# Router logits with the weights stationary on two halves of TensorE's columns, in a hybrid decoder layer

## The reference, cut to what matters

```python
x = x + h                                    # h: the mixer's output, @ w_out
xn = rms_norm(x, norm_ffn)
p_group = softmax(x32 @ w_router_group + b_router_group)     # 4 groups
fine = x32 @ w_router_expert + b_router_expert               # 32 experts
...                                          # best group, best two experts of it, their gates
```

## Time and profile before

| what | value |
|---|---|
| median of 3 runs | 1838.29 us (1837.46 to 1838.7) |
| the profiled execution | 1837.38 us, its span 1835.7 us |
| PE busy | 1771.8 us, 97% of the span |
| DVE busy | 1151.4 us, 63% |
| ACT busy | 863.1 us, 47% |
| chain that ended last, PE's share of the span | 36%, of it L2379 1% |

### The profile page before, as it was taken

How to read it: one execution, slowest core, us unless ns; L and a number is a source line. 1 busy time by engine, 2 the same in 40 slices (tenths; PEclk the granted TensorE clock), 3 DMA queues, 4 the chain that set the end, 5 groups by cost and what they waited for, 6 DMA issues and landing times. The chain is left out here.

```text
span 1835.7 us, 28478 instructions
## 1 busy us (share of the span) xinstructions
PE 1771.8 (97%) x9926; PEld 1529.7 (83%) x9926; DVE 1151.4 (63%) x1954; ACT 863.1 (47%) x1554; POOL 485.7 (26%) x495
## 2 busy tenths in 40 slices
PE   7989999999999999999999999979999999999997
PEld 6878888999999888888878978758888888888883
DVE  5267665311111354545456556689999999999985
ACT  5255555311111223332223223358787778778873
POOL 3022332000000232323231112223965333333320
PEclk9989999999999999999999999979999999999998
DMA  7121211332213203030204643279999999999987
GB/s 225 54 50 43 56 47 47 94 93 65 76 52 95 69 27 92 23 94 23 95 1 132 192 142 124 91 286 381 396 385 384 392 387 385 383 383 387 384 338 292
DMA packets 149531, 333.30 MB, mean 182 GB/s; under 512 B 33712, under 2 KB 103008, under 8 KB 123792
## 3 DMA queue, kind: packets, MB, share of 16 engines
q1 hardware_dynamic: 127408, 278.19, 41.7%
q0 software_dynamic: 21376, 53.27, 8.4%
q10 hardware_dynamic: 672, 0.85, 0.3%
HBM read 304.24 MB, written 46.35 MB: 191 GB/s over the span
## 5 line engine op out<-in xcount | busy, mean ns | idle before, releaser
L2832 POOL DMA_INDIRECT y_d<-e_y,e_idxs x32 | 138.4, 4325 | 201.4 <-DVE e_y L2938 179.8
L2909 DVE TENSOR_TENSOR e_Lg<-e_rawg,e_Hg 128x1024 fp32r<-128x1024 f32 x128 | 148.3, 1219 | 8.3 <-ACT e_Hg L2858 8.3
L2909 DVE TENSOR_TENSOR e_Lu<-e_rawu,e_Hu 128x1024 fp32r<-128x1024 f32 x128 | 147.8, 1213 | 0.0
L2909 DVE TENSOR_TENSOR e_Ld<-e_rawd,e_Hd 128x1024 fp32r<-128x1024 f32 x124 | 143.1, 1213 | 0.0
L2858 ACT ACTIVATE e_Hg<-e_rawg 128x1024 fp32r<-128x1024 f32 x128 | 124.7, 1051 | 9.2 <-DMA e_rawg<-in_w_gate 9.2
L2858 ACT ACTIVATE e_Hu<-e_rawu 128x1024 fp32r<-128x1024 f32 x124 | 121.0, 1059 | 0.0
L2858 ACT ACTIVATE e_Hd<-e_rawd 128x1024 fp32r<-128x1024 f32 x124 | 120.7, 1051 | 0.0
L164 PE MATMUL bank<-r_wH,xH 128*128 128x512 f32 x256 | 105.9, 414 | 2.4 <-DVE r_gs L1512 2.4
L164 PE MATMUL bank<-e_Hg,e_xH 128*128 128x512 f32 x256 | 100.8, 394 | 3.5 <-DVE e_xL L2915 3.5
L164 PE MATMUL bank<-e_Hu,e_xH 128*128 128x512 f32 x256 | 102.8, 402 | 0.0
L166 PE MATMUL bank<-r_wH,xL 128*128 128x512 f32 x256 | 101.5, 397 | 0.0
(11 more groups left out here) (464 smaller groups left out, 4774.6 us busy)
## 6 DMA issues: line engine op xcount, KB each, us to landing
e_rawg<-in_w_gate SPq DMA_DIRECT2D x64, 1024.0 KB, 8.6
e_rawu<-in_w_up SPq DMA_DIRECT2D x64, 1024.0 KB, 7.5
e_rawd<-in_w_down SPq DMA_DIRECT2D x62, 1024.0 KB, 8.1
raw<-in_w_in SPq DMA_DIRECT2D x51, 512.0 KB, 4.0
c_Y<-y_d SPq DMA_DIRECT2D x8, 1024.0 KB, 12.2
m_t<-b_m_s POOLq DMA_DIRECT2D x8, 528.0 KB, 3.4
m_gate<-gate_t POOLq DMA_DIRECT2D x8, 528.0 KB, 4.0
m_m<-m_t POOLq DMA_DIRECT2D x8, 528.0 KB, 3.9
```

What stands on the lines that cost most here:

```text
L2832: pool.indirect_dma_start(out=ch.y_d, out_offset=bass.IndirectOffsetOnAxis(ap=idx[:, e % IDX, 1:2], axis=0), in_=y[:], in_offset=None, bou ...
L2909: dve.tensor_tensor(L[kind][:, q], raw[kind][:, q], H[kind][:, q].bitcast(F32), ALU.subtract).then_inc(w_lo[kind], 1)
```

## The change

The roles in the router product are swapped. The weights `wr`, padded from 40 to 64 columns, are stationary, and the turned tokens move (128 columns). The eight slices of the contraction go in turn to the lower and the upper half of the columns (`PART`), so bank 6 holds two partial sums of the transposed logits, of the even slices in partitions 0 to 63 and of the odd ones in 64 to 127. ScalarE copies them to SBUF (`parts_out`). A new step `join` on PE multiplies them by `halves`, two identities of 40 columns one above the other (rows 0 to 39 and 64 to 103), which adds the halves and turns the logits back to one row a token. DVE reads them from another place of bank 6. In the loop the join stands behind two more slices of the projection, and two slices follow it. The waits for `r_mm` that guarded the turned rows are for `part_mm` now.

```diff
-        wr, rb = sb("o_wr", [P, KT, NL]), sb("o_rb", [P, NL])
+        wr, rb = sb("o_wr", [P, KT, P // 2]), sb("o_rb", [P, NL])
...
+        parts, halves = aside("o_parts", [P, P]), aside("o_halves", [P, NL])
+        PART = [slice(r * P // 2, (r + 1) * P // 2) for r in range(2)]
...
+            def parts_out(t):
+                m = rows_of(t)
+                act.wait_ge(part_mm, t + 1)
+                act.activation(parts[:, 0:m], banks[6][:, 0:m], ACT.Copy).then_inc(part_out, 1)
...
             for t in range(1, NT):
                 back(t - 1)
+                parts_out(t - 1)
                 front(t)
...
             back(NT - 1)
+            parts_out(NT - 1)
             split_hi("g", range(NQ))
...
             dve.memset(wr[:, :, NG:EPG], 0.0).then_inc(pad_done, 1)
+            dve.memset(wr[:, :, NL:], 0.0).then_inc(pad_done, 1)
+            dve.tensor_tensor(halves[:], ch.ident[:, 0:NL], ch.ident[:, P // 2:P // 2 + NL], ALU.add).then_inc(pad_done, 1)
...
-                dve.tensor_tensor(lg[0:m], banks[6][0:m, 0:NL], rb[0:m], ALU.add).then_inc(lg_done, 1)
+                dve.tensor_tensor(lg[0:m], banks[6][0:m, P:P + NL], rb[0:m], ALU.add).then_inc(lg_done, 1)
...
                 pe.wait_ge(t_out0, t + 1)
                 pe.wait_ge(t_out1, t + 1)
+                for k in range(KT):
+                    mm = pe.matmul(banks[6][PART[k % 2], 0:m], wr[:, k, :], xT[:, k, 0:m], start=(k < 2), stop=(k >= KT - 2))
+                mm.then_inc(part_mm, 1)
+
+            def join(t):
+                m = rows_of(t)
+                pe.wait_ge(part_out, t + 1)
                 pe.wait_ge(lg_done, t)
-                for k in range(KT):
-                    mm = pe.matmul(banks[6][0:m, 0:NL], xT[:, k, 0:m], wr[:, k, :], start=(k == 0), stop=(k == KT - 1))
-                mm.then_inc(r_mm, 1)
+                pe.matmul(banks[6][0:m, P:P + NL], parts[:, 0:m], halves[:], start=True, stop=True).then_inc(r_mm, 1)
...
-                project(t, 1, 0)
+                project(t, 1, range(KT // 2))
                 if t >= 1:
                     route(t - 1)
-                project(t, 1, 1)
+                project(t, 1, range(KT // 2, KT * 3 // 4))
+                if t >= 1:
+                    join(t - 1)
+                project(t, 1, range(KT * 3 // 4, KT))
...
             route(NT - 1)
             enlist(NT - 3, 1)
+            join(NT - 1)
             enlist(NT - 2, 1)
```

More of the change, by code:

```diff
@@ L1985, in output_programs @@
     mm_half, xn_half = sem("o_mmh"), sem("o_xnh")
+    part_mm, part_out = sem("o_pmm"), sem("o_pout")
     x2_st, xn_st, turned, t_out0, t_out1, r_mm = ([sem("o_x2s0"), sem("o_x2s1")], [sem("o_xns0"), sem("o_xns1")], sem("o_t"), sem("o_to0"), sem("o_to1"),
@@ L2047, in gpsimd @@
         def gpsimd(pool):
-            for dst, src in ((gain[:], ch.norm_ffn.broadcast_to([P, D])), (wr[:, :, 0:NG], ch.w_rg), (wr[:, :, EPG:], ch.w_re),
+            for dst, src in ((gain[:], ch.norm_ffn.broadcast_to([P, D])), (wr[:, :, 0:NG], ch.w_rg), (wr[:, :, EPG:NL], ch.w_re),
                              (rb[:, 0:NG], ch.b_rg.broadcast_to([P, NG])), (rb[:, EPG:], ch.b_re.broadcast_to([P, NE]))):
@@ L2097, in back @@
                 act.wait_ge(turned, t * 2 + 1)
-                act.wait_ge(r_mm, t)
+                act.wait_ge(part_mm, t)
                 act.activation(xT[:, 0:4, 0:m], banks[4][:].rearrange("p (k i) -> p k i", k=4)[:, :, 0:m], ACT.Copy).then_inc(t_out0, 1)
+            def parts_out(t):
+                m = rows_of(t)
+                act.wait_ge(part_mm, t + 1)
+                act.activation(parts[:, 0:m], banks[6][:, 0:m], ACT.Copy).then_inc(part_out, 1)
             def exponentials(t):
@@ L2133, in vector @@
             dve.wait_ge(tab_in, 16 * 5)
-            dve.wait_ge(pad_done, 4)
+            dve.wait_ge(pad_done, 6)
             count = [0]
@@ L2191, in back @@
                 dve.wait_ge(turned, t * 2 + 2)
-                dve.wait_ge(r_mm, t)
+                dve.wait_ge(part_mm, t)
                 dve.tensor_copy(xT[:, 4:8, 0:m], banks[5][:].rearrange("p (k i) -> p k i", k=4)[:, :, 0:m]).then_inc(t_out1, 1)
@@ L2335, in tensor, with project @@
         def tensor(pe):
-            def project(t, f, half=None):
+            def project(t, f, ks=range(KT)):
                 m, s = rows_of(t), t % 2
@@ L2339, in project @@
                     pe.wait_ge(add_done, t - 1)
-                for k in range(KT) if half is None else range(half * KT // 2, (half + 1) * KT // 2):
+                for k in ks:
                     if t == 0 and f == 0 and k < KT - 1:
@@ L2350, in project @@
                                        (out.H[f][:, k], out.L[f][:, k]), k == 0, k == KT - 1)
-                if f == NH - 1 and half == 1:
+                if f == NH - 1 and ks[-1] == KT - 1:
                     mm.then_inc(mm_done, 1)
@@ L2372, in route @@
                     pe.wait_ge(tab_in, 16 * 5)
-                    pe.wait_ge(pad_done, 4)
+                    pe.wait_ge(pad_done, 6)
                     pe.wait_ge(table_in, 16 * 7)
```

## The result

The changed kernel takes 1847.12 us (median of 5 runs, 1845.58 to 1849.93), the kernel before 1838.7 us in the same sitting (5 runs, 1837.46 to 1840.87). The ratio is 1.0041, 95% interval 1.003 to 1.0051: slower by 0.3 to 0.5%. The forecast was 1846.5 us, 8.2 us more than before.

What follows compares the result with a forecast made beforehand. PE's work and an equally long ring through DVE and ACT were taken to bound the loop together. Loop 7.4, tile 7 0.1 and last route 0.7 made +8.2 us, 1846.5 us; eight-in-ten range 1842 to 1851.5.

Steps and rivals of the forecast that it cites:

- The bound: Tile loop: PE's own work and the chain through DVE and ACT end together at 14.20 us, neither with slack.
- the handoff of 0.15 us: From the end of DVE's normalization to PE's transposes: 0.15 us in the loop, the same as behind tile 7's recorded wait.
- The router product: On PE: column halves run side by side, 1.11 us until the projection goes on, against 1.71 before.
- The rival that weight loads stand in the way of the other half: Router product: 64-column loads stand in each pair, 0.44 us in nine tiles, 3.9 us, 1850.4 us; chance 0.05.
- The logits: After the join: ready 2.97 us from the router product's slot against 1.92, so 1.05 us later in every tile.
- The ring: Loop of logits, DVE and ACT, transposes, twelve matmuls, router product: 1.05 us longer at seven turns, 7.4 us.
- The waits: PE before each tile's transposes: idle for the normalization, 1.4 us each and 2.9 at tile 7.
- The tail: Tile 7's logits 0.44 us late, of which 0.1 comes through; last tile's route at half clock adds 0.7 us.
- a rival with a chance of 0.06: PE's clock granted at half after tile 7's idle time: fourteen projection matmuls cost 3.2 us, 1849.7 us; chance 0.06.
- Absorbed: Half the needed slack exists or expert transfers don't shift: within 3.7 us of now, say 1840; chance 0.05.
- not slower: Loop: transposes have at least 1.40 us of slack and PE alone is the bound: -2.1, 1836.2 us; chance 0.06.

Runs made afterwards that it cites:

- The delay alone: Kernel before with the router product moved behind six slices of project(t, 1) instead of four, no work added: 1850.56 us, ratio 1.0063.
- the moved `choose` in the kernel before: Kernel before with choose(t - 1) on DVE moved behind front(t) instead of ahead of it: 1841.24 us, ratio 1.0006.
- the single-half kernel: Changed kernel with all eight slices on the lower column half, copy and join on 64 partitions: 1856.9 us, ratio 1.0096.
- the kernel with three edits: Changed kernel with choose(t - 1) behind front(t), join behind one projection slice, last tile routed with rows stationary, without copy or join: 1838.71 us, ratio 0.9995.
- the join at once: Changed kernel with the join right behind the partial products, no projection matmul between: 1843.14 us, ratio 1.0017.
- the last tile in the old form: Changed kernel with only tile 8 routed with rows stationary and weights moving, without copy or join: 1848.09 us, ratio 1.0043.
- `choose` moved in the changed kernel: Changed kernel with choose(t - 1) on DVE moved behind front(t) instead of ahead of it: 1838.9 us, ratio 0.999.

## Why the prediction was right, point by point

**The bound.** That the handoff of 0.15 us was a wait that the profile doesn't record, and PE and ring ended together, carried everything else. The delay alone and the moved `choose` in the kernel before show it, one from each side: 1.39 us more in the ring cost 1.22 us a tile, 1.4 us less won nothing.

**The router product.** Forecast 0.09 before the block and 1.02 to the projection; measured 0.10 and 1.02. L920 was the right row to price it from. The rival that weight loads stand in the way of the other half is refuted by the same 1.02 us. Here the Trainium skill's rule (TensorE: Matmul & The Clock Gate, Part 3, "The mechanism"), that a load overlaps matmuls in flight only when its row group differs, does not agree with the trace: the single-half kernel, too, kept 0.109 us a record with a load for each. The same section of the Trainium skill also lets a load into the background weight buffer run ahead; the prediction had left that out.

**The logits.** Forecast 2.97 us from the slot; measured 2.97 (from 1139.09, where the next step was due 0.232 us after the projection matmul at 1138.86, to L2212 at 1142.06). So 1.05 us late, as forecast.

**The ring.** Forecast 1.05 us a tile and 7.4 in seven; measured 0.90 and 6.3. The term was mis-sized where the text held the 8.45 us of DVE and ACT unchanged: they are 1148.21+2.14-1142.06 = 8.29. The normalization is 0.16 us shorter where PE stands idle beside it (last section). At tile 7, where PE stood idle beside it before as well (2.07 us long then, 2.05 now), the tile did grow by the full term, 1.04 us.

**The waits.** Forecast 1.4 us at each turn and 2.9 at tile 7; measured 1.09 and 2.86. The 0.31 us at each turn are two terms. The normalization is shorter by 0.16. The second is a matter of reading: the recorded wait begins where the last counting record ends, 0.39 us after its start, but matmuls are pipelined. In the kernel before, where the transposes start at 1145.48, that record starts only 0.24 us before them:

```profile
1145.24 0.39 PE L2388 MATMUL bank<-t_cum,t_ones 128*128 128x32 f32 x2
```

So a recorded wait is 0.15 us short of what it costs. By the starts it costs 1150.50-1149.02-0.24 = 1.24 us, and 15.10-1.24 = 13.86 is PE's own work, 0.34 less than before, where 0.35 were forecast. At tile 7 both kernels waited, so neither term shows there.

**The tail.** Forecast 0.8 us; measured 1.7. The last tile's route costs 1.97 instead of 1.38 us to the logits, 0.6 more where 0.7 were forecast. Tile 7's logits come 2.34 us behind the first record instead of 1.98, 0.36 late (forecast 0.44), and the next turn follows them after 7.62 us instead of 8.01, so that nothing comes through, where 0.1 us was forecast. What the sum lacked is the clock: the forecast kept it at 1.00 and had its fall as a rival with a chance of 0.06, and a part of that rival happened. The timeline and the table of stretches of the changed kernel:

```profile
1195.66 1.21 PE L2378 MATMUL bank<-identity,o_xns 128*128 128x128 f32 x8 [2.86 <-DVE o_xns L2198]
...
1197.10 0.63 PE L172 MATMUL bank<-o_wL,m_xS 128*64 128x512 f32 x1
1197.53 0.63 PE L171 MATMUL bank<-o_wH,m_xS 128*64 128x512 f32 x1
...
1200.08 1.09 PE L2390 MATMUL bank<-o_xT,o_wr 128*64 128x128 f32 x16
```

```profile
1196.50:1199.90 3.40, 3.40 (x11) 1.73 (x8) 3.12 (x12) 0.61 (x2) 1.52 (x2) 0.51 0.38 154
1199.90:1206.00 6.10, 4.66 (x39) 3.57 (x38) 3.55 (x15) 0.79 (x2) 0.89 (x2) 1.00 0.29 70
```

Behind the 2.86 us of idleness the clock is granted at half (1.2 GHz) for 3.4 us and a projection matmul steps by 0.43 us instead of 0.23. From turn to partial products are 4.42 us instead of 3.35: 1.07 us, a third of the rival's 3.2, because only eight projection matmuls fell in the stretch, not fourteen, and part of their length lies where PE had stood idle for 0.43 us before.

The errors of ring and tail, -1.1 and +0.9 us, nearly cancel: 8.0 instead of 8.2 us in the stage. That the total is so close is in part luck.

**Absorbed, not slower.** Neither happened: the turns moved apart, and behind the last logits the changed kernel and the kernel before take 630.1 and 630.3 us.

## What to carry to other kernels

An engine at 100% with no recorded wait may still be held by a ring that is exactly as long as its work. Compare the handoff's distance with one where the wait is recorded; if they are equal, anything that delays the ring costs nearly its full length in every pass, and a saving of PE's work is worth nothing until the ring is cut as well. The distance is a hint and no proof: in the kernel before with `choose` moved it is 0.18 us, little more than 0.15, though the logits have slack. What decides is an experiment that delays the ring and adds no work, and one that shortens it.

When an intermediate result is split in two steps so that other work covers the copy between them, the cover is paid by whoever waits for the result. Put behind the copy only as much as covers it (three matmuls here, not six), or take off the waiting chain what it doesn't need (`choose`, 1.4 us). Three are a tight cover: in the kernel with three edits the copy ended only 0.12 us before the join began.

## What the runs showed of the hardware

**DVE's normalization takes longer beside a busy PE.** The table of groups gives the mean of the normalization's six in the loop, 128x1024 each, with the same operands. In the kernel before, PE is busy throughout; in the changed kernel and in that with the delay alone it is idle for 1.09 us, the last 0.94 us of the instruction and the 0.15 of the handoff; with the join behind one slice for 0.47 us:

```profile
L2186 DVE SCALAR_TENSOR_TENSOR o_xns<-o_x2s,o_stat,o_gain 128x1024 f32<-128x1024 f32 x6 | 13.8, 2304 | 0.2
```

```profile
L2198 DVE SCALAR_TENSOR_TENSOR o_xns<-o_x2s,o_stat,o_gain 128x1024 f32<-128x1024 f32 x6 | 12.8, 2136 | 0.2
```

2304, 2236, 2136 and 2137 ns for 0, 0.47, 1.09 and 1.09 us of idle PE; with the join at once, where PE doesn't wait at the turn, 2302. The length goes with PE's idle time at about 0.15 us per us. It is a correlation in one instruction. GpSimd had no instruction beside it in either kernel: its last one before ends at 1142.07 against 1143.03 and at 1147.25 against 1148.21. What DVE and PE share was not tried.

**The clock behind a wait is not a matter of its length alone.** It fell behind the wait at tile 7 in the changed kernel (2.86 us) and with the last tile in the old form (2.86), with one half (2.72) and with the join behind one slice (2.17), and held in the kernel before (1.48), with `choose` moved in the changed kernel (1.51) and the join at once (1.51), but also with the delay alone, at 2.87 us. What else decides stays open.
